# Level scores of HGRN and GLA in narrow products, and retention scores of two heads together

## The reference, cut to what matters

```python
att = jnp.einsum('bhid,bhjd->bhij', qc, kc) * intra
o = jnp.einsum('bhij,bhjv->bhiv', att, vc) + jnp.einsum('bhid,bhdv->bhiv', qc * q_dec, s)
```

```python
def chunk_gla(q, k, v, g):
    """S_t = diag(exp(g_t)) S_{t-1} + k_t v_t^T ; o_t = S_t^T q_t (per-key-channel decay)."""
    ...
    rel = jnp.exp(jnp.where(incl, G_c[..., :, None, :] - G_c[..., None, :, :], -jnp.inf))
    a = jnp.einsum('bhcd,bhsd,bhcsd->bhcs', q_c, k_c, rel)
```

## Time and profile before

| | us |
|---|---|
| median of 3 runs | 2466.81 |
| lowest and highest | 2459.60, 2469.43 |
| the profiled execution | 2464.71 |
| its span, first to last instruction | 2462.9 |
| TensorE busy | 2408.8 |
| VectorE busy | 1760.4 |
| ScalarE busy | 1175.4 |

### The profile page before, as it was taken

How to read it: one execution, slowest core, us unless ns; L and a number is a source line. 1 busy time by engine, 2 the same in 40 slices (tenths; PEclk the granted TensorE clock), 3 DMA queues, 4 the chain that set the end, 5 groups by cost and what they waited for, 6 DMA issues and landing times.

```text
span 2462.9 us, 47920 instructions
## 1 busy us (share of the span) xinstructions
PE 2408.8 (98%) x18258; PEld 2230.0 (91%) x18258; DVE 1760.4 (71%) x2908; ACT 1175.4 (48%) x1819; POOL 75.8 (3%) x149
## 2 busy tenths in 40 slices
PE   8999999999999999989999999999999999989998
PEld 6877877778988999988999998999989999988998
DVE  5788799988847876786666868665567667776665
ACT  5454522233645444566444555444545446466444
POOL 1000000000000000000300000000000000000000
PEclk9999999999999999999999999999999999999999
DMA  8433355554524565422655522555424554322653
GB/s 315 158 108 128 112 181 194 180 181 157 178 90 145 195 183 169 131 92 70 197 182 184 178 88 78 196 182 186 147 87 161 187 174 162 110 87 80 202 175 133
DMA packets 119708, 378.20 MB, mean 154 GB/s; under 512 B 11655, under 2 KB 29063, under 8 KB 119184
## 3 DMA queue, kind: packets, MB, share of 16 engines
q1 hardware_dynamic: 107040, 328.62, 40.6%
q0 software_dynamic: 12528, 47.62, 5.8%
HBM read 375.15 MB, written 1.05 MB: 153 GB/s over the span
## 4 chain that ended last, share of the span: by engine, by line
PE 78%; DVE 11%; issue 6%; ACT 3%; DMA 1%; DVEq 1%; SPq 0%; ACTq 0%
PE gb L608 20%; PE gb L610 19%; PE gb L609 19%; DVE w_lo L577 2%; PE mb L3010 2%; PE mb L717 1%; DVE W L1627 1%; PE mb L608 1%; PE mb L609 1%; PE mb L610 1%; DVE W L2738 1%; PE gb L2991 1%; DMA X<-in_x 1%; ACT w_hi L569 1%; DVE W L1251 1%
## 5 line engine op out<-in xcount | busy, mean ns | idle before, releaser
L608 PE MATMUL gb<-Xs,w_hi 128*128 128x256 f32 (+1 forms) x3422 | 1037.5, 303 | 10.2 <-DVE w_lo L577 4.9
L610 PE MATMUL gb<-Xs,w_lo 128*128 128x256 f32 (+1 forms) x3422 | 1022.0, 299 | 0.0
L609 PE MATMUL gb<-Xs,w_hi 128*128 128x256 f32 (+1 forms) x3336 | 993.2, 298 | 0.0
L569 ACT ACTIVATE w_hi<-raw 128x1024 fp32r<-128x1024 f32 x582 | 610.6, 1057 | 691.4 <-PE gb L610 650.9
L577 DVE TENSOR_TENSOR w_lo<-raw,w_hi 128x1024 fp32r<-128x1024 f32 x582 | 705.9, 1223 | 210.8 <-ACT w_hi L569 203.8
L608 PEld LDWEIGHTS gb<-Xs,w_hi 128*128 128x128 f32 x3422 | 644.8, 188 | 57.8 <-issue 17.5
L610 PEld LDWEIGHTS gb<-Xs,w_lo 128*128 128x128 f32 x3422 | 645.2, 189 | 26.0
L609 PEld LDWEIGHTS gb<-Xs,w_hi 128*128 128x128 f32 x3336 | 629.3, 189 | 23.4 <-issue 1.9
L609 PE MATMUL gb<-Fs,w_hi 128*128 128x256 f32 (+1 forms) x966 | 278.2, 288 | 0.0
L608 PE MATMUL gb<-Fs,w_hi 128*128 128x256 f32 (+1 forms) x880 | 248.9, 283 | 0.7 <-ACT Pj L1776 0.7
L610 PE MATMUL gb<-Fs,w_lo 128*128 128x256 f32 (+1 forms) x880 | 247.1, 281 | 0.0
(11 more groups left out here) (469 smaller groups left out, 3287.2 us busy)
## 6 DMA issues: line engine op xcount, KB each, us to landing
raw<-in_up SPq DMA_DIRECT2D x264, 512.0 KB, 3.3
raw<-in_down SPq DMA_DIRECT2D x96, 512.0 KB, 3.7
R<-in_mod_later POOLq DMA_DIRECT2D x80, 512.0 KB, 3.6
raw<-in_gdn_in SPq DMA_DIRECT2D x64, 512.0 KB, 3.3
raw<-in_down SPq DMA_DIRECT2D x48, 384.0 KB, 4.0
raw<-in_hgrn_in SPq DMA_DIRECT2D x32, 512.0 KB, 4.2
raw<-in_ev_in SPq DMA_DIRECT2D x24, 512.0 KB, 4.2
raw<-in_gla_in SPq DMA_DIRECT2D x24, 512.0 KB, 4.0
```

The lines of the kernel that those rows point to most:

```text
L569: nc.scalar.activation(hi, raw[:, slot, 0:hi.shape[1]] if len(hi.shape) == 3 else like(raw[:, slot], hi), ACT.Identity).then_inc(*hi_ready ...
L608: nc.tensor.matmul(to, weight_block(w_slot, 0, k), x_hi, start=start, stop=False)
L609: nc.tensor.matmul(to, weight_block(w_slot, 0, k), x_lo, start=False, stop=False)
L610: return nc.tensor.matmul(to, weight_block(w_slot, 1, k), x_hi, start=False, stop=stop)
```

## The change

Level scores: levels 0 to 4 become 32 products of 32 keys by 16 queries each (every 32 keys with the queries of the same 32 tokens), level 5 16 products of 32 keys by 32 queries, level 6 eight products of 64 keys by 64 queries. Each writes only its own partitions (32 or 64) of the bank. Level 7 is as before. Levels 5 and 6 are no longer copied by VectorE with a mask but by ScalarE, as whole rectangles (two for level 5, one for level 6), after the exponentials of the unit two later. Two semaphores are new, and TensorE waits for both kinds of copy before it writes a bank again. Retention: the scores of heads 0 and 1 are multiplied together before `pair(0, T)`, with the products alternating between the two row halves, those of heads 2 and 3 inside `pair(2, T)`.

```diff
-            def score(h):
-                rows = slice(64 * (h % 2), 64 * (h % 2) + 64)
-                if h == 0:
+            def score_two(g):
+
+                if g == 0:
                     pe.wait_ge(*roped.seen("pe"))
-                if h >= 2:
-                    pe.wait_ge(*mixed.due("pe"))
+                else:
+                    pe.wait_ge(*mixed.due("pe", 2))
                 for k in range(4):
-                    last = nc.tensor.matmul(score_banks[2 * (h % 2) + k // 2][:, (k % 2) * T:(k % 2 + 1) * T],
-                                            Pj[rows, 2 + h // 2, k * P:(k + 1) * P], Pj[rows, h // 2, 0:T], start=True, stop=True)
+                    for odd in range(2):
+                        rows = slice(64 * odd, 64 * odd + 64)
+                        last = nc.tensor.matmul(score_banks[2 * odd + k // 2][:, (k % 2) * T:(k % 2 + 1) * T],
+                                                Pj[rows, 2 + g, k * P:(k + 1) * P], Pj[rows, g, 0:T], start=True, stop=True)
                 last.then_inc(*scores.inc())
...
-            score(0)
-            pair(0, T, {0: lambda: score(1)})
-            pair(2, T, {0: lambda: score(2)})
-            pair(0, 2 * T, {0: lambda: score(3), 1: pool_tokens, 3: pool_features})
+            score_two(0)
+            pair(0, T, {})
+            pair(2, T, {0: lambda: score_two(1)})
+            pair(0, 2 * T, {1: pool_tokens, 3: pool_features})
...
-                dve.wait_ge(*scores.due("dve"))
+                if h % 2 == 0:
+                    dve.wait_ge(*scores.due("dve"))
...
+        HIGH = (LEVELS - 2, LEVELS - 1)
...
+            def banks_free(u):
+                high = sum(l in HIGH for l in levels_of(z.units[u][1]))
+                pe.wait_ge(*mixed.due("pe", 2 - high))
+                if high:
+                    pe.wait_ge(*high_placed.due("pe", high))
+
             def level_scores(u):
...
-                    if l < LEVELS:
+                    if l < LEVELS - 1:
+                        per, n = (2, 32) if l == LEVELS - 2 else (4, 16)
                         for b in range(8):
-                            last = nc.tensor.matmul(bank[:, b * 64:(b + 1) * 64], keys[:, b, :], queries[:, b * 64:(b + 1) * 64],
+                            for m in range(per):
+                                rows, cols = slice(P // per * m, P // per * m + 32), slice(b * 64 + n * m, b * 64 + n * m + n)
+                                last = nc.tensor.matmul(bank[rows, cols], keys[:, b, rows], queries[:, cols], start=True, stop=True)
+                    elif l == LEVELS - 1:
+                        for b in range(8):
+                            last = nc.tensor.matmul(bank[0:64, b * 64:(b + 1) * 64], keys[:, b, 0:64], queries[:, b * 64:(b + 1) * 64],
                                                     start=True, stop=True)
...
-                    last.then_inc(*scores.inc())
+                    last.then_inc(*(high_scores if l in HIGH else scores).inc())
...
-                    pe.wait_ge(*mixed.due("pe", 2))
+                    banks_free(u - 2)
...
         def act_gla_core(act, z):
+
+            def place_high(u):
+                g, pair = z.units[u]
+                for l in levels_of(pair):
+                    if l not in HIGH:
+                        continue
+                    if l == HIGH[0]:
+                        act.wait_ge(*mixed.due("act", z.heads // 4 + 5 if g == 0 else 6))
+                    act.wait_ge(*high_scores.due("act"))
+                    to = z.own[:, 8 * g:8 * g + 8, :]
+                    made = score_bank(u, l).rearrange("p (b i) -> p b i", b=8)
+                    for m in range(LEVELS - l):
+                        rows = slice(64 * m, 64 * m + (1 << l))
+                        last = nc.scalar.activation(to[rows, :, rows.stop:rows.stop + (1 << l)], made[rows, :, m << l:(m + 1) << l], ACT.Identity)
+                    last.then_inc(*high_placed.inc())
...
+                if u >= 2:
+                    place_high(u - 2)
             level_rows.due("act", 4)
+            for u in (-2, -1):
+                place_high(len(z.units) + u)
...
             def place(u):
                 g, pair = z.units[u]
                 for l in levels_of(pair):
+                    if l in HIGH:
+                        continue
                     dve.wait_ge(*scores.due("dve"))
```

More of the change, by code:

```diff
@@ L330, in build @@
         gate_log = signal("gate_log")
+        high_scores = signal("high_scores")
+        high_placed = signal("high_placed")
         gate_turned = signal("gate_turned")
@@ L3033, in pe_gla_core @@
             pe.wait_ge(*spans_exp.due("pe", 2))
-            pe.wait_ge(*mixed.due("pe", 4))
+            for u in (-2, -1):
+                banks_free(len(z.units) + u)
             w = D // z.heads
@@ L3060, in act_gla_core @@
                         split_hi(act, ahead["act"].next())
+                if u >= 2:
+                    place_high(u - 2)
             level_rows.due("act", 4)
+            for u in (-2, -1):
+                place_high(len(z.units) + u)
+            mixed.due("act")
             def square(c):
@@ L3066, in act_gla_core @@
             gn_roots(act, z.items, parts=z.parts, square=square)
-            mixed.due("act", z.heads // 4 + 2 * len(z.units))
         def dve_gla_core(dve, z):
```

## The result

The changed kernel takes 2449.15 us, the median of five runs (2444.53 to 2454.04), against 2466.81 for the kernel before in the same job: a ratio of 0.9942, 95% interval 0.9922 to 0.9963, so 9 to 19 us faster. A second set of six runs, in a later job, gave 2448.40 against 2465.49, 0.9934 [0.9914, 0.9953]. The forecast was 2450. The execution that was profiled is the slowest of the five: 2454.04 us, with a span of 2452.3 against 2462.9 before.

What follows compares the result with a forecast made beforehand. TensorE was taken to bound the kernel, with VectorE next in line in the cores. Cores -13.4, retention -3.8 and clock +1.0 gave -16.2 us, from 2464.71 to 2448.5 profiled and 2450 as the median, range 2443 to 2465.

Steps and rivals of the forecast that it cites:

- What bounds the kernel, and overlap of narrow passes: Whole kernel: TensorE bounds it, busy 98% of the span; in the level scores, narrow passes overlap by two.
- Rival (a): Level scores: narrow passes don't overlap, 30 ns each, 0.0 per group; only retention's -3.8 left, 2463 us; chance 0.33.
- 10.6 and 5.3: HGRN and GLA cores: microseconds of TensorE work saved by the level scores, -5.3 us per group.
- The price of a pass: Level scores: a pass of 32 key columns costs 15 ns, levels 0 to 4 take 0.96 us each.
- lower bound of 7.5: Level scores: nanoseconds per narrow pass if all four column quarters run together, 30 / 4.
- The 58 ns for level 6: Level 6 scores: 16 passes one after another at 58 ns, 0.93 us, saving 0.83 us.
- HGRN -8.9, GLA -4.5: Both cores: elapsed gain in us after charging 1.4 and 0.8 for imperfect fit of TensorE and VectorE; together -13.4.
- has nearly no idle left: HGRN core: sign that the forecast is right, VectorE almost never idle and the core 36 to 39 us.
- Clock, +1.0: Cores and retention: none to four falls at 1.5 us each, one in retention perhaps gone (-1.5); net +1.0 us.
- Copies by ScalarE: Levels 5 and 6: ScalarE gains 1.3 us per group, hidden in its idle time; VectorE loses 1.5 us per group.
- VectorE's ceiling: Both cores: VectorE's remaining work limits the gain to at most -10.3 us in HGRN and -5.4 in GLA.
- Retention, -3.8: Retention scores: alternating row halves let 16 passes take 1.92 to 2.13 us, saving 3.8 us, without a stall.

Runs made afterwards that it cites:

- turned loops: The change with the loops over blocks and key quarters exchanged, so eight products of one column quarter follow each other; 2455.74 us, ratio 0.9953.
- shifted code: The change with 36 level-0 products of each core's first unit issued again, 72 passes more, same result; 2458.32 us, one run.
- halves: The change with levels 0 to 5 in products of 64 keys by 32 queries, two a block; 2445.39 us, ratio 0.9916.
- levels alone: The change with its retention edit taken back, keeping narrow level scores and ScalarE's copies; 2452.98 us, ratio 0.9949.
- retention alone: The kernel before with only the change's edit of the retention scores; 2457.65 us, ratio 0.9977.

## Why the prediction came out right

The number was right, 2450 against 2449.15, and so was the kind of cause; the sum behind it was right only in part, and errors of both signs met. Point by point:

**What bounds the kernel, and overlap of narrow passes.** Right. Rival (a), at 0.33, was the one to rule out, and the turned loops do so: 26 ns in sequence, 8.7 side by side. TensorE's busy time fell by 10.3 and 5.4 us in the cores, where the working had 10.6 and 5.3, but that it fits so well is luck: the passes were cheaper than forecast, and the lower clock made the rest longer. In shifted code, where HGRN's core is at full clock, busy time is 33.4 us; without the 0.6 of its repeats that is a fall of 13.0. The Trainium skill's rule in "TensorE: Matmul & The Clock Gate", Part 3, that weight loads overlap running matmuls only where the row group differs, doesn't describe these products: same rows, other columns, a third of the time.

**The price of a pass.** Mis-sized: 15 ns taken, 8.7 measured, near the lower bound of 7.5. Two quarters at once had been read from rows with two parts; it is about three. A unit of levels 0 and 1 takes 1.11 us where 1.9 was forecast. This error made the change look dearer than it is. The "60 cycles" a matmul of the Trainium skill's page "TensorEngine Tiling (Array Packing)", Instruction Overhead, an estimate of 25 ns, meet the passes in one quarter (26 ns) but not those side by side. The 58 ns for level 6 was right (0.92 us from the first to the last of 16 starts, 58 each but for the first step), and so was a tenth of a microsecond for a change of shape (0.21 us from the start of the last exponent pass to the first narrow one, where the exponent passes ahead of it start 1.86 / 15 = 0.124 us apart).

**HGRN -8.9, GLA -4.5.** This step failed in the profiled execution. The core was to take 36 to 39 us and took 41.84. Measured from first exponent to the end of the tail: HGRN -4.8 in the core and +2.2 behind it, so -2.6; GLA -3.3. What stands in its place is three things that the working had not, or not there. First a pause of 2.5 us (1.4 in GLA) in which TensorE waits for its instructions, a supply that no row of before showed as short. Second, VectorE is late as forecast, but in one place, the last ten microseconds of the core, and not as an engine that is never idle: it works 32.5 of 41.8 us. Of its 9.3 us of idle time 3.3 lie ahead of its first instruction, as forecast, and 6.1 behind it, so the forecast's sign that VectorE "has nearly no idle left" didn't come. In the halves 2.8 us lie behind it: there VectorE is close to the bound that the forecast saw. Third, the clock falls behind the pause and in the wait for VectorE. The halves, with neither pause nor fall, take 38.5 and 21.0 us: -8.2 and -4.3, where the working had -8.9 and -4.5. Their level costs 0.92 us as well, the forecast's 0.96. So the sum described a kernel without the pause, and the change isn't quite that one.

**Clock, +1.0.** Mis-sized. That small pauses bring falls was said, and three of them stand in or behind the cores of the profiled execution. By the tail (2.24 us for 4.6 us at the lower clock) a microsecond at that level costs half a microsecond there. So the price of 1.5 us is about right for the two falls of 3.4 us, but the third lasted 10.2 us; the 17.1 us together cost some 8 at most, and less where TensorE wasn't the bound. In all, the time at the lower clock went from 41.7 to 52.7 us.

**Copies by ScalarE.** Hidden, as said, and the gain on the other side, 1.5 us of VectorE a group, is hidden as well: with the copies back on VectorE nothing changes. The forecast counted them into VectorE's ceiling, which wasn't reached.

**Retention, -3.8.** Right: -4.2, 16 passes in 1.93 us, no stall at the second pair. The extra 1.5 from the clock came in this execution too, and also without this part.

**The sum.** For the profiled execution 2448.5 was forecast, and it took 2454.04, 5.5 us more: the cores came out 7.5 us dearer than forecast (-2.6 - 3.3 against -13.4), retention 1.9 better with its clock, and the rest of the program 1.0 slower, as much as the clock term had allowed. The median lies 4.9 below that execution. That it met the forecast so closely is luck of about that size; that it is faster, by nearly 0.4 per cent at the least in both sets of runs, is not. And a range of 2443 to 2465 doesn't tell the forecast's mechanism from no overlap at all, which the turned loops put at 2456: the trace does that, not the time.

## What to carry to other kernels

Where most of a product isn't wanted, four times as many small ones can take a third of the time (1.11 us for 128 passes instead of 3.52 for 32), if neighbours in the instruction order use different columns: put the loop over the column groups innermost. Then look at TensorE's timeline for idle time that no semaphore ends, and at the row of the instruction queue; where it appears, half as many products of twice the size can win in that stretch although TensorE works longer. And look at what the clock does behind every hole of one or two microseconds, since the bill for a short wait can come after it. Last, look at the mechanism in the trace and not at the time alone: here a change of the loops that makes the passes three times dearer moved the ratio of the whole program from 0.9942 to 0.9953, each within the other's interval.

## What the runs showed of the hardware

- Full-row passes of 32 columns by 16: 8.7 ns each with four column quarters in turn, 26 ns in one quarter; 64 columns by 32, two halves in turn, 29 ns; 64 columns by 64 in one half, 58 ns.
- With passes of 8.7 ns TensorE stood still for 1.2 to 2.5 us, at places a multiple of 256 of its records apart (give or take one), which repeated from one execution to another, and went on 2.3 to 2.6 us after the start of an instruction packet. With 26 or 29 ns it didn't stand still. How many instructions are held ahead of it, and who else shares their supply, stays open.
- In or behind pauses of 1.4 to 2.5 us and waits of 2.0 us in these cores the granted clock was at its lower level for 3.4 to 10.2 us. After one pause of 2.19 us (levels alone), pauses and waits of 1.2 to 1.7 (shifted code, HGRN) and waits of 1.2 (the halves) it wasn't. The unchanged GLA core of retention alone fell too (28.48 us instead of 25.33), and why is open.
